# Two attentions of a fused three-layer block: a pair's sums over the values move one step later, between a step's scores and its turning

## The chip, the cores and the metric

The program runs on one core of one Trainium2 chip. The metric is the device time of one execution in microseconds (us). An execution is some 2.1 ms long, and the two attentions that the change touches take 75 us and 82 us of it.

## What is computed

The reference is a chain of three transformer layers on one sequence of 512 positions of width 1024, all in float32. The first layer has a sparse attention with 8 query heads of 64 over 2 groups of keys, a retention and an MLP. The second has an mLSTM, the third a softmax attention with 16 heads of 64 and a gate (called fox), and both have a feed-forward part. Two of its attentions count here:

```python
# first layer: selected blocks (with 8 blocks all are selected) and a window of 512, so both are causal attention
ss = jnp.einsum('qghd,gqkd->gqhk', qi, k_sel).astype(jnp.float32) * scale
p_s = jax.nn.softmax(jnp.where(smask, ss, NEG), axis=-1)
o_s = jnp.einsum('gqhk,gqkd->qghd', p_s.astype(dt), v_sel)
...
# third layer
logits = jnp.einsum('bqhd,bkhd->bhqk', qi, k).astype(jnp.float32)
logits = logits + (ci[..., :, None] - c[..., None, :])
p = jax.nn.softmax(jnp.where(mask, logits, -jnp.inf), axis=-1)
return jnp.einsum('bhqk,bkhd->bqhd', p.astype(v.dtype), v)
```

## The kernel before

Activations lie transposed in SBUF (128 features by 512 positions a tile). Weights stream in and are split in a high and a low part, and a product is three matmuls (L409 to L411). Each engine has one written-out order of instructions, and the engines are tied by counting semaphores. No planner decides anything: the order in the text is the order of issue.

Both attentions are one function, `attention` (L1110). The first layer's is called at L1632 (below: the first attention, 148 to 223 us of the trace), fox's at L2698 (1618 to 1700 us). The work of one attention is cut into 8 **pairs** of heads, and each pair into 4 **units**: unit i of a pair (i = 0 to 3) has the 128 queries of block i, and the (i + 1) x 128 keys that they may see, for both heads e = 0, 1 of the pair. So there are 32 units, of widths 128, 256, 384 and 512 in turn. A unit goes through these hands:

- `score` on TensorE (L1166, in fox also L2686, and L1171 for the mask): scores of both heads into two PSUM banks. Four banks serve two units, so `score(u)` waits until the exponentials of unit u - 2 have read theirs (`probs_ready`). With i = 0 it also waits for the split queries (`staged`).
- `maximum` on VectorE (L1230): the negated row maximum, one instruction a head.
- `exponential` on ScalarE (L1296): exp with the row sum beside it, one activation and one reading of the accumulator a head.
- `weigh` on VectorE (L1237, L1244 in the first attention, L1242 in fox): the probabilities times the reciprocal row sum.
- `turn` on TensorE (L1183): i + 1 transposes a head into one of two banks. It waits for `weighted`, and for ScalarE's copy of the last unit out of the same bank.
- `copy` on ScalarE (L1308, L1306): the turned probabilities into SBUF.
- `values` on TensorE (L1196): once a pair, after its unit i = 3, sixteen matmuls that sum over the values. It waits for the pair's last copy.
- `take` on VectorE (L1631 in the first attention, where two pairs add up in one bank and only every second pair is taken, L2681 in fox): the sums out of PSUM.

Once a pair, in the step with i = 0, ScalarE makes the high part of the next pair's queries (in fox of the keys too) at L1273, and VectorE the low part at L1213. In fox ScalarE also copies the values of a pair into `total` or `inv` (`stage_values`, L1288), and waits there for the sums of the pair before last.

The software pipeline is in `steps`: in step s each engine runs its `step` function once, and `unit(d)` is unit s - d. ScalarE's step is, in this order: the high parts (if i = 0), `copy(s - 3)`, `exponential(s)`, `stage_values`. VectorE's is `maximum(s)`, the low parts (if i = 0), `weigh(s - 1)`, then `take`. A step is named below by the width of its score: the 128 step is the one with i = 0.

Of the kernel before, what the change touches and what calls it, by code (L numbers as in the profile page):

```python
# [183 lines left out]
def build(nc, io, at):  # L184
    top = ExitStack()
    with top:
# [181 lines left out]
        def finish(spec):  # L368
            for b in range(spec.blocks):
                slot = (stream["slot"] + b) % 2  # L370
                raw_loaded[slot].n += 16
            stream["slot"] = (stream["slot"] + spec.blocks) % 2
            for t in (hi_ready, lo_ready, products_done):
                t.n += spec.blocks
# [735 lines left out]
        def attention(turns_n, q_of, k_of, v_of, static, space, factor, finish, together, lent, probs, free, key_bias=None, ends=None):  # L1110
# [12 lines left out]
            def turned_keys(p, e, j):  # L1123
                return probs_t[p][e][:, j, j * P:S] if j < 3 else probs_t[p][e][:, 1, 0:P]
# [12 lines left out]
            def prob(u, e):  # L1137
                return probs[2 * (u % 3) + e]

            def column(x, u, e):  # L1140
                return x[u % 3][:, e:e + 1]

            def steps(lag, step):
                for s in range(units + lag):
                    step(s, lambda lead: s - lead if 0 <= s - lead < units else None)

            def last_of(u):
                return u is not None and u % U == U - 1

            def tensor(pe):  # L1150
                def score(u):
                    n, i = u // U, u % U
                    w = (i + 1) * P
                    q, k = held[n]
                    half = [slice(64 * e, 64 * e + 64) for e in range(2)]
                    out = [score_bank[2 * (u % 2) + e] for e in range(2)]
                    if u < 2:

                        pe.wait_ge(evacuated.sem, b_e - 1 + u)
                    if i == 0:  # L1160
                        pe.wait_ge(staged.sem, b_st + once + each * (n + 1))
                    if u >= 2:
                        pe.wait_ge(probs_ready.sem, b_p + 2 * (u - 1))
                    for a, b in ((0, 0), (0, 1), (1, 0)):
                        for e in range(2):
                            pe.matmul(out[e][:, 0:w], q[a][half[e], i * P:w], k[b][half[e], 0:w],  # L1166
                                      start=a == 0 and b == 0, stop=False)
                    if key_bias is not None:
                        key_bias(pe, out, n, w)
                    for e in range(2):  # L1170
                        last = pe.matmul(out[e][:, i * P:w], ident_b[:, :], bias_b[:, :], start=False, stop=True)  # L1171
                    last.then_inc(scores_ready.sem, 1)

                def turn(u):
                    if u == 0:
                        pe.wait_ge(rows_out.sem, b_ro)
                        pe.wait_ge(cmp_dve.sem, b_cd)
                    for e in range(2):
                        pe.wait_ge(weighted.sem, b_n + 2 * u + e + 1)
                        if u >= 1:  # L1180
                            pe.wait_ge(probs_copied.sem, b_c + 2 * u + e - 1)
                        for j in range(u % U + 1):
                            last = pe.transpose(turn_bank[e][:, j * P:(j + 1) * P], prob(u, e)[:, j * P:(j + 1) * P], ident)  # L1183
                        last.then_inc(probs_turned.sem, 1)

                def values(u):
                    n, p = u // U, u // U % 2
                    pe.wait_ge(probs_copied.sem, b_c + 2 * u + 2)
                    if n >= 2:
                        pe.wait_ge(out_done.sem, b_d + (n // 2 if together else n - 1))  # L1190
                    out = out_bank[0 if together else p]
                    vals = v_of(n) if static else v_st[p]
                    for j in range(TT):
                        for e in range(2):
                            rows = slice(64 * e, 64 * e + 64)
                            last = pe.matmul(out[rows, j * P:S], vals[:, j, rows], turned_keys(p, e, j),  # L1196
                                             start=j == 0 and not (together and p == 1),
                                             stop=j == TT - 1 and not (together and p == 0))
                    last.then_inc(out_ready.sem, 1)

                def step(s, unit):
                    if unit(0) is not None:
                        score(unit(0))
                    if unit(3) is not None:
                        turn(unit(3))
                    if last_of(unit(4)):
                        values(unit(4))
                steps(5, step)

            def stage_low(dve, n):  # L1210
                for r, (st, src) in enumerate(stagings(n)):
                    dve.wait_ge(high_staged.sem, b_hi + once + n * each + r + 1)
                    dve.tensor_tensor(st[1], src, st[0].bitcast(F32), ALU.subtract).then_inc(staged.sem, 1)  # L1213
# [9 lines left out]
            def vector(dve):  # L1223
                def maximum(u):
                    w = (u % U + 1) * P
                    dve.wait_ge(scores_ready.sem, b_s + u + 1)
                    for e in range(2):
                        if u >= 3:
                            dve.wait_ge(probs_ready.sem, b_p + 2 * u + e - 5)
                        dve.tensor_reduce(column(neg_max, u, e), score_bank[2 * (u % 2) + e][:, 0:w], AX_X, ALU.max,  # L1230
                                          negate=True).then_inc(max_ready.sem, 1)

                def weigh(u):
                    n, i = u // U, u % U
                    w = (i + 1) * P
                    dve.wait_ge(probs_ready.sem, b_p + 2 * u + 2)
                    dve.reciprocal(row_sum[u % 3][:, :], row_sum[u % 3][:, :])  # L1237
                    dve.drain()  # L1238
                    for e in range(2):
                        x, scale = prob(u, e)[:, 0:w], column(row_sum, u, e)  # L1240
                        if factor is None:
                            ins = dve.tensor_scalar(x, x, scale, None, ALU.mult)  # L1242
                        else:
                            ins = dve.tensor_scalar(x, x, scale, factor(n, e, i), ALU.mult, ALU.mult)  # L1244
                        ins.then_inc(weighted.sem, 1)

                def take(u):
                    n, p = u // U, u // U % 2
                    if together and p == 0:
                        return  # L1250
                    if ends is not None and n == pairs - 1:
                        ends(dve)
                    dve.wait_ge(out_ready.sem, b_o + n + 1)
                    finish(dve, n, out_bank[0 if together else p]).then_inc(out_done.sem, 1)

                def step(s, unit):
                    if unit(0) is not None:
                        maximum(unit(0))
                        if s % U == 0 and s // U + 1 < pairs:
                            stage_low(dve, s // U + 1)  # L1260
                    if unit(1) is not None:
                        weigh(unit(1))
                    if last_of(unit(5)):
                        take(unit(5))
                steps(6, step)

            def stage_high(act, n):
                if n == 1:
# [58 lines left out]
            out_ready.n += pairs  # L1327
            out_done.n += turns_n if together else pairs
            return {"tensor": tensor, "vector": vector, "scalar": scalar}, begin_act, begin_dve

        def region(off, *shape):
# [1450 lines left out]
```

## Time and profile before

| what | value |
|---|---|
| median of 3 runs | 2143.31 us (2141.17 to 2144.65) |
| the profiled execution's own time | 2142.03 us |
| its span, first to last instruction | 2140.2 us |
| TensorE (PE) busy | 2066.3 us, 97% |
| VectorE (DVE) busy | 1220.8 us, 57% |
| ScalarE (ACT) busy | 795.5 us, 37% |
| mean granted TensorE clock | 0.987 |

The page's shares are means over some two dozen stages. Most of the span is streamed dense products that keep TensorE busy without a gap, and they hide that in the two attentions ScalarE and VectorE are busy nearly all the time too. For a change in the attentions the timelines of these stretches have to be read.

### The profile page before, as it was taken

Reading aid. Unit: us, or ns where it says so; the run is one execution under the profiler, and the core shown is the slowest. Engines: PE = TensorE matmul, PEld = TensorE weight load, DVE = VectorE, ACT = ScalarE, POOL = GpSimd, SP = SyncE. Lnnn points to the kernel's source line nnn. Section 1 sums busy time; section 2 is a strip of 40 time slices with the busy share of each in tenths; the row PEclk is TensorE's granted clock in tenths of the full one; section 3 lists DMA queues with packets and bytes.
Section 4 is the critical chain, followed back from the end, with each engine's and each line's share of the span. In section 5 each row is a group of like instructions: output and inputs, shape, how many; then the busy total and the mean of one; then the engine's idle time right before and its main releaser. Section 6 shows DMA issues by size and latency. Waiting matters only on the chain.

```text
span 2140.2 us, 25567 instructions
## 1 busy us (share of the span) xinstructions
PE 2066.3 (97%) x9936; PEld 1674.0 (78%) x9944; DVE 1220.8 (57%) x1719; ACT 795.5 (37%) x1236; POOL 21.3 (1%) x45
## 2 busy tenths in 40 slices
PE   7899999999999999999999999999999999999996
PEld 6776778888888888877788888878786678888885
DVE  5669645455444355456575564663537757647375
ACT  4239243232212133245343342442427734323242
POOL 1000000000000000000000000000000000000000
PEclk9989999999999999999999999999999999999998
DMA  4410412222222222321122223222220022222221
GB/s 168 158 60 1 128 50 93 104 99 99 99 98 99 99 98 77 120 89 59 60 98 98 98 79 113 70 94 89 99 99 21 21 79 79 98 98 98 99 83 54
DMA packets 34240, 188.52 MB, mean 88 GB/s; under 512 B 4440, under 2 KB 8696, under 8 KB 14400
## 3 DMA queue, kind: packets, MB, share of 16 engines
q1 hardware_dynamic: 31296, 179.41, 23.8%
q0 software_dynamic: 1696, 5.72, 1.0%
q10 hardware_dynamic: 1152, 2.10, 0.3%
q8 instruction: 62, 1.02, 0.2%
q14 instruction: 34, 0.28, 0.0%
HBM read 182.54 MB, written 2.11 MB: 86 GB/s over the span
## 4 chain that ended last, share of the span: by engine, by line
PE 88%; DVE 5%; ACT 2%; issue 1%; DVEq 1%; PEld 1%; DMA 1%; PEldq 0%; POOL 0%; SPq 0%; ACTq 0%; POOLq 0%
PE bank L409 23%; PE bank L411 23%; PE bank L410 23%; PE bank L486 4%; PE bank L491 4%; PE bank L487 4%; PE bank L1196 2%; PE bank L1166 1%; PE bank L645 1%; DVE w_lo L357 1%; PE bank L2205 1%; PE bank L1183 1%; ACT w_hi L343 1%; PE bank L2197 1%; DVEq L1238 0%
## 5 line engine op out<-in xcount | busy, mean ns | idle before, releaser
L343 ACT ACTIVATE w_hi<-w_raw 128x2048 fp32r<-128x2048 f32 (+3 forms) x174 | 314.4, 1807 | 812.0 <-PE bank L411 689.6
L409 PE MATMUL bank<-a_hi,w_hi 128*128 128x512 f32 x1376 | 540.3, 393 | 3.7 <-DVE shared L2546 1.6
L411 PE MATMUL bank<-a_hi,w_lo 128*128 128x512 f32 x1376 | 536.5, 390 | 0.0
L410 PE MATMUL bank<-a_lo,w_hi 128*128 128x512 f32 x1376 | 536.5, 390 | 0.0
L357 DVE TENSOR_TENSOR w_lo<-w_raw,w_hi 128x2048 fp32r<-128x2048 f32 (+3 forms) x174 | 374.8, 2156 | 143.7 <-ACT w_hi L343 143.5
L409 PEld LDWEIGHTS bank<-a_hi,w_hi 128*128 128x128 f32 x1376 | 258.9, 188 | 60.0 <-issue 3.4
L411 PEld LDWEIGHTS bank<-a_hi,w_lo 128*128 128x128 f32 x1376 | 258.8, 188 | 54.2
L410 PEld LDWEIGHTS bank<-a_lo,w_hi 128*128 128x128 f32 x1376 | 259.0, 188 | 53.3 <-issue 0.2
L409 PE MATMUL bank<-big_halves,w_hi 128*128 128x512 f32 x616 | 240.6, 391 | 3.1 <-DVE w_lo L357 3.0
L411 PE MATMUL bank<-big_halves,w_lo 128*128 128x512 f32 x616 | 239.8, 389 | 0.0
L410 PE MATMUL bank<-big_halves,w_hi 128*128 128x512 f32 x616 | 239.7, 389 | 0.0
L409 PEld LDWEIGHTS bank<-big_halves,w_hi 128*128 128x128 f32 x616 | 115.6, 188 | 29.7 <-DVE w_lo L357 5.9
L411 PEld LDWEIGHTS bank<-big_halves,w_lo 128*128 128x128 f32 x616 | 115.6, 188 | 24.2
L410 PEld LDWEIGHTS bank<-big_halves,w_hi 128*128 128x128 f32 x616 | 115.6, 188 | 23.8
L409 PE MATMUL bank<-w_hi,a_hi 128*128 128x512 f32 (+1 forms) x288 | 111.0, 385 | 3.0 <-DVE big L1676 1.0
L411 PE MATMUL bank<-w_hi,a_lo 128*128 128x512 f32 (+1 forms) x288 | 109.1, 379 | 0.0
L410 PE MATMUL bank<-w_lo,a_hi 128*128 128x512 f32 (+1 forms) x288 | 109.0, 379 | 0.0
L2546 DVE TENSOR_TENSOR shared<-bank,inv 128x512 f32<-128x512 f32 x88 | 56.6, 686 | 71.8 <-PE bank L411 71.5
L486 PE MATMUL bank<-a_hi,w_hi 128*128 128x512 f32 x176 | 74.3, 422 | 21.1 <-DVE w_lo L995 12.0
L2534 ACT ACTIVATE shared<-shared,conv 128x512 f32<-128x512 f32 x88 | 66.5, 803 | 34.1 <-DVE shared L2546 34.1
L2537 ACT ACTIVATE shared<-shared 128x512 f32<-128x512 f32 x44 | 27.9, 634 | 122.1 <-DVE shared L2556 122.1
L486 PE MATMUL bank<-big_halves,w_hi 128*128 128x512 f32 x184 | 72.2, 392 | 0.0
(340 smaller groups left out, 2432.6 us busy)
## 6 DMA issues: line engine op xcount, KB each, us to landing
w_raw<-in_w_fu SPq DMA_DIRECT2D x44, 1024.0 KB, 4.8
w_raw<-in_w_up SPq DMA_DIRECT2D x16, 1024.0 KB, 4.8
w_raw<-in_w_down SPq DMA_DIRECT2D x16, 1024.0 KB, 4.8
w_raw<-in_w_fd SPq DMA_DIRECT2D x16, 1024.0 KB, 4.8
w_raw<-in_w_fd SPq DMA_DIRECT2D x8, 768.0 KB, 4.3
w_raw<-in_w_rqk SPq DMA_DIRECT2D x4, 1024.0 KB, 5.0
w_raw<-in_w_rvg SPq DMA_DIRECT2D x4, 1024.0 KB, 5.0
w_raw<-in_w_gate SPq DMA_DIRECT2D x4, 1024.0 KB, 4.8
```

The costliest lines, as they stand in the source:

```text
L343: act.activation(w_hi[slot][:, cols], raw[slot][:, cols], ACT.Copy).then_inc(hi_half_ready.sem if half == 0 else hi_ready.sem, 1)
L357: ins = dve.tensor_tensor(w_lo[slot][:, cols], raw[slot][:, cols], w_hi[slot][:, cols].bitcast(F32), ALU.subtract)
L409: pe.matmul(out, w[0], x[0], start=first, stop=False)
L410: pe.matmul(out, w[0], x[1], start=False, stop=False)
L411: return pe.matmul(out, w[1], x[0], start=False, stop=last)
L486: pe.matmul(bank[2 * slot + c][:, :], w[0], x[0], start=k == 0, stop=False)
L487: pe.matmul(bank[2 * slot + c][:, :], w[1], x[0], start=False, stop=False)
L491: last = pe.matmul(bank[2 * slot + c][:, :], weights(slot, col)[0], x[1], start=False, stop=final)
L1196: last = pe.matmul(out[rows, j * P:S], vals[:, j, rows], turned_keys(p, e, j), start=j == 0 and not (together and p == 1), stop=j == TT - ...
L2534: act.activation(z[slot][:, c, :], u[slot][:, c, 2:S + 2], ACT.Identity, scale=tap(2, b, c), bias=tap(3, b, c)).then_inc(tapped.sem, 1)
L2537: act.activation(z[slot][:, 0, :], z[slot][:, 0, :], ACT.Gelu_apprx_tanh).then_inc(gelu_ready.sem, 1)
L2546: ins = dve.tensor_tensor(u[slot][:, c, 2:S + 2], bank[2 * slot + c][:, :], inv[:, :], ALU.mult)
```

## The change

The kernel's own time table in `step` is changed on two engines. On TensorE `values` was the last thing of a step, for the unit four behind the one just scored. Now it stands between `score` and `turn`, for the unit five behind. On VectorE `take` is one step later, six behind instead of five. Both loops get one step more at the end.

```diff
@@ tensor @@
                 def step(s, unit):
                     if unit(0) is not None:
                         score(unit(0))
+                    if last_of(unit(5)):
+                        values(unit(5))
                     if unit(3) is not None:
                         turn(unit(3))
-                    if last_of(unit(4)):
-                        values(unit(4))
-                steps(5, step)
+                steps(6, step)
@@ vector @@
                     if unit(1) is not None:
                         weigh(unit(1))
-                    if last_of(unit(5)):
-                        take(unit(5))
-                steps(6, step)
+                    if last_of(unit(6)):
+                        take(unit(6))
+                steps(7, step)
```

What this moves on TensorE in the first attention, at the end of a pair's 512 step (L1196 `values`, L1166 and L1171 `score`, L1183 `turn`):

```order
 L1171 MATMUL bank<-bias_b,ident_b 128x128 x2
 L1183 MATMUL bank<-const_sb,work 128x128 x2
+L1166 MATMUL bank<-big_halves 128x128 x6
+L1171 MATMUL bank<-bias_b,ident_b 128x128 x2
 L1196 MATMUL bank<-big,shared 64x512 x2
 L1196 MATMUL bank<-big,shared 64x384 x2
 L1196 MATMUL bank<-big,shared 64x256 x2
 L1196 MATMUL bank<-big,shared 64x128 x2
-L1166 MATMUL bank<-big_halves 128x128 x6
-L1171 MATMUL bank<-bias_b,ident_b 128x128 x2
 L1183 MATMUL bank<-const_sb,big 128x128 x4
```

The eight score matmuls of the next pair's 128 step now come before the sixteen of the sums, and the four transposes of unit i = 1 come after both. There are six such places in each attention (pairs 0 to 5). The sums of pair 6 stand in a step without a score: they move from behind the turning of unit 28 to before that of unit 29, which is the same place, and the last pair's sums stay last.

On VectorE in fox, before, from the low parts (L1213) of one pair's 128 step on:

```order
L1213 TENSOR_TENSOR a_lo<-big,a_hi 128x512 x2
L1237 RECIPROCAL row_sum<-row_sum 128x2
L1242 TENSOR_SCALAR a_plain<-a_plain,row_sum 128x512 x2
L2681 TENSOR_TENSOR big<-bank,big 128x512
L1230 TENSOR_REDUCE neg_max<-bank 128x1 x2
L1237 RECIPROCAL row_sum<-row_sum 128x2
L1242 TENSOR_SCALAR work<-work,row_sum 128x128 x2
L1230 TENSOR_REDUCE neg_max<-bank 128x1 x2
```

And with the change:

```order
L1213 TENSOR_TENSOR a_lo<-big,a_hi 128x512 x2
L1237 RECIPROCAL row_sum<-row_sum 128x2
L1242 TENSOR_SCALAR a_plain<-a_plain,row_sum 128x512 x2
L1230 TENSOR_REDUCE neg_max<-bank 128x1 x2
L1237 RECIPROCAL row_sum<-row_sum 128x2
L1242 TENSOR_SCALAR work<-work,row_sum 128x128 x2
L2681 TENSOR_TENSOR big<-bank,big 128x512
L1230 TENSOR_REDUCE neg_max<-bank 128x1 x2
```

The take (L2681) goes from before the 256 step's maximum to before the 384 step's. Nothing moves on ScalarE, GpSimd or the queue of SyncE.

## Rows read from the trace of the kernel before

**Rows 1.** The page: busy time, share of the span and instructions of each engine.

```profile
PE 2066.3 (97%) x9936; PEld 1674.0 (78%) x9944; DVE 1220.8 (57%) x1719; ACT 795.5 (37%) x1236; POOL 21.3 (1%) x45
```

**Rows 2.** Busy time by window: from the third pair's 128-wide score to the last pair's.

```profile
core 0: us, PE busy (x) PEld busy (x) DVE busy (x) ACT busy (x) POOL busy (x), PEclk, DMA share, GB/s
165.91:208.17 42.26, 40.94 (x342) 26.64 (x340) 38.08 (x108) 38.30 (x137) 0.00 (x0) 1.00 0.01 2
1635.13:1683.89 48.76, 45.18 (x377) 29.76 (x380) 40.93 (x115) 42.81 (x145) 0.00 (x0) 1.00 0.01 2
```

**Rows 3.** Timeline, first attention: start, duration, engine, instruction, count, [idle before <-releaser].

```profile
163.60 2.38 PE L1196 MATMUL bank<-big,shared 128*64 128x512 f32 x16
...
164.10 0.25 ACT L1296 ACTIVATION_READ_ACCUMULATOR work<-bank,neg_max 128x1 f32 x1
...
165.91 0.55 PE L1166 MATMUL bank<-big_halves 64*128 64x128 f32 x6
...
166.72 0.49 DVE L1230 TENSOR_REDUCE neg_max<-bank 128x1 f32<-128x128 f32 x2 [0.52 <-PE bank L1171]
166.94 0.66 ACT L1308 ACTIVATE shared<-bank 128x256 f32<-128x256 f32 x2 [0.36 <-PE bank L1183]
...
167.61 0.29 PE L1171 MATMUL bank<-bias_b,ident_b 128*128 128x128 bf16 x2
...
168.26 0.87 ACT L1308 ACTIVATE shared<-bank 128x384 f32<-128x384 f32 x2
...
168.88 0.75 DVE L1230 TENSOR_REDUCE neg_max<-bank 128x1 f32<-128x256 f32 x2
...
169.33 0.47 ACT L1296 ACTIVATE work<-bank,neg_max 128x256 f32<-128x256 f32 x1 [0.19 <-DVE neg_max L1230]
...
172.32 0.25 ACT L1296 ACTIVATION_READ_ACCUMULATOR work<-bank,neg_max 128x1 f32 x1
```

**Rows 4.** Timeline, first attention's last pair: its 128-wide score and its sums.

```profile
208.17 0.55 PE L1166 MATMUL bank<-big_halves 64*128 64x128 f32 x6
...
220.50 2.37 PE L1196 MATMUL bank<-shared 128*64 128x512 f32 x16 [0.86 <-ACT shared L1308]
```

**Rows 5.** Timeline, fox: pair 0's sums and what stands at their end.

```profile
1632.83 2.38 PE L1196 MATMUL bank<-fx_probs_t,total 128*64 128x512 f32 x16
1632.92 0.32 ACT L1296 ACTIVATION_READ_ACCUMULATOR work<-bank,neg_max 128x1 f32 x1
...
1635.13 0.33 PE L1166 MATMUL bank<-a_hi 64*128 64x128 f32 x2
```

**Rows 6.** Timeline, fox, one pair further on.

```profile
1642.58 2.37 PE L1196 MATMUL bank<-fx_probs_t,inv 128*64 128x512 f32 x16
...
1644.89 0.33 PE L1166 MATMUL bank<-a_hi 64*128 64x128 f32 x2
...
1646.03 0.73 ACT L1308 ACTIVATE fx_probs_t<-bank 128x256 f32<-128x256 f32 x2 [0.34 <-PE bank L1183]
...
1646.93 0.27 PE L1171 MATMUL bank<-bias_b,ident_b 128*128 128x128 bf16 x2
...
1647.87 0.88 ACT L1308 ACTIVATE fx_probs_t<-bank 128x384 f32<-128x384 f32 x2
...
1649.50 0.47 ACT L1296 ACTIVATE work<-bank,neg_max 128x256 f32<-128x256 f32 x1 [0.75 <-DVE neg_max L1230]
...
1650.57 0.50 PE L1166 MATMUL bank<-a_hi 64*128 64x512 f32 x2 [0.57 <-ACT work L1296]
...
1652.49 0.25 ACT L1296 ACTIVATION_READ_ACCUMULATOR a_plain<-bank,neg_max 128x1 f32 x1
```

**Rows 7.** Chain of waits in fox, merged: start, length, what (a steady pair's middle).

```profile
1645.81 0.29 DVE neg_max L1230
1646.30 1.20 DVE a_lo L1213 x2
1647.91 0.62 DVEq L1238
1648.53 0.60 DVE big L2681
```

**Rows 8.** Busy time by window: granted clock (PEclk) at the first attention's start and after.

```profile
147.00:158.00 11.00, 8.38 (x52) 5.49 (x51) 7.38 (x19) 6.47 (x19) 0.00 (x0) 0.71 0.01 2
...
166.00:225.00 59.00, 56.10 (x452) 36.65 (x453) 48.09 (x135) 49.60 (x173) 1.81 (x4) 1.00 0.02 5
```

## The prediction

> **What bounds the kernel now.** The page comes first: TensorE is busy 97% of the span [rows 1]. That is the mean of a kernel that is mostly dense products. The windows of busy time over the attentions say more: over five pairs TensorE is busy 40.94 of 42.26 us in the first attention and 45.18 of 48.76 us in fox, while ScalarE is busy 38.30 and 42.81 us [rows 2]. So TensorE waits 1.32 and 3.58 us there, some 0.26 and 0.72 us a pair, and ScalarE is close behind. Two engines at nine tenths mean that a loop through both decides, and for that I read the timelines.
>
> In fox the loop is plain. The sums run from 1642.58, and the next pair's 128 score can start only behind them, at 1644.89 [rows 6]. The chain of waits then goes over VectorE: maximum, low parts, weighing of unit 3, the take [rows 7]. Only then comes the 256 maximum, for which ScalarE has stood idle 0.75 us, and for its exponentials the 512 score has waited 0.57 us [rows 6]. After the 512 score come two transposes and the next sums, and the circle is closed: (1683.89 - 1635.13) / 5 = 9.75 us a pair. The first attention has the same circle with fewer instructions in it. ScalarE's wait for the 256 maximum is 0.19 us in a pair with no take before it [rows 3], and a pair takes 42.26 / 5 = 8.45 us [rows 2].
>
> **What the change does to the circle.** The sums (2.31 us from their start to the next start, 163.60 to 165.91 [rows 3]) leave the place ahead of the 128 score and go behind it, ahead of the turning of unit 1. No instruction is added. The 128 score is now held only by the 384 exponentials two units before, and VectorE's chain starts earlier. But the turning of unit 1 is late, ScalarE's copy of it waits, and queued behind that copy in the same in-order stream are the 128 exponentials and all that follow. So the new circle is: 128 score, sums, turning of unit 1, then ScalarE without a pause through copy 1, exponentials 128, copy 2, exponentials 256, copy 3, exponentials 384, which let the next 128 score go.
>
> *The first attention's steady pair.* From the 128 score's start to copy 1 it is 166.94 - 165.91 = 1.03 us now [rows 3], and 1.03 + 2.31 = 3.34 us with the sums between. ScalarE's string runs from 166.94 to the end of the 384 exponentials at 172.32 + 0.25 = 172.57, less the idle 0.19 us: 5.44 us [rows 3]. With 0.05 us for the signal that is 8.83 us. I take 8.8, since an idle time counts from the end of a record, and ScalarE's instructions otherwise start a little before the last one's record ends. Five pairs: 44.0 against 42.26, **+1.7 us**.
>
> *Its head.* The 128 score of the third pair starts at 165.91, behind the sums of the first. Without them it can start when the 384 exponentials are read, 164.10 + 0.25 + 0.05 = 164.40 [rows 3]: **-1.5 us**.
>
> *Its tail.* At the last pair's 128 score (208.17) the sums of pairs 0 to 5 are done today. With the change those of pair 5 are still to do, so from there to the end at 222.87 [rows 4] TensorE has 2.31 us more to do, and its only waits in the first half are of 0.1 to 0.3 us: **+2.1 us**. Together the first attention loses 2.3 us.
>
> *Fox.* Steady pair: copy 1 comes 1646.03 - 1644.89 = 1.14 us after the 128 score, with the sums 3.45. ScalarE's string from 1646.03 to 1652.74, less the 0.75 us of idle time that falls away, is 5.96 us [rows 6]. The sum with the signal is 9.46, and I take 9.4 by the same correction. Five pairs: 47.0 against 48.76, **-1.8 us**. Head: 1635.13 becomes 1632.92 + 0.32 + 0.05 = 1633.29 [rows 5], **-1.8 us**. Tail: 2.31 us of sums more, with TensorE without a wait, **+2.3 us**. Together fox gains 1.3 us.
>
> *The copy of values in fox.* ScalarE's `stage_values` waits for the sums of the pair before last. They now end only after the 128 score, but before the turning for which ScalarE has already waited in copy 1 of the same step. It costs nothing, and if the order were otherwise it would cost what copy 1 costs, once.
>
> *The take.* It waits for sums that end 3.1 us after the 128 score starts, and VectorE reaches it some 6 us after. Cost nothing. It leaves the way of the 256 maximum (0.60 us [rows 7]), and that is the reason why the 0.75 us in fox goes. What comes before the 384 maximum is unchanged in sum.
>
> *Outside.* The stages behind each attention shift with its end. No load is issued inside. Nothing.
>
> **Sum: +2.3 - 1.3 = +1.0 us.** Each half of that trade is worth more than the net. The profiled execution took 2142.03 us, its median over three runs is 1.3 us higher. I count from the middle, 2142.7, and forecast **2143.7 us**. A measurement here can tell some 0.2%, 4.3 us, from no change.
>
> *Bounds.* Low: TensorE never waits in the steady pairs. Then they give -1.3 and -3.6 instead of +1.7 and -1.8, and the sum is +1.0 - 3.0 - 1.8 = -3.8 us, 2138.9. High: ScalarE keeps its waits for the 256 maximum, 0.19 and 0.75 us a pair, on top of the new circle: 5 x (8.83 + 0.19) = 45.1 and 5 x (9.46 + 0.75) = 51.1, which is +2.8 and +2.3, and the sum is -1.5 + 2.8 + 2.1 - 1.8 + 2.3 + 2.3 = +6.2 us, 2148.9.
>
> *A rule against this working.* By occupancy TensorE is the fullest engine of the first attention, 40.94 us against ScalarE's 38.30 [rows 2], and by the timeline it is the circle through both that closes last. The Trainium skill (Perfetto Trace Analysis: Identifying the Most-Contended Engine) says to take the engine with the highest occupancy as the bottleneck, though it warns that matmul busy time is no good measure of TensorE. If that were all, the sums could stand anywhere in TensorE's order, and the first attention's steady pairs would gain their 1.3 us instead of losing 1.7.
>
> **The rivals.**
>
> 1. *TensorE is the bound in the first attention*, and ScalarE makes up for its late start. The new circle leaves TensorE only 8.8 - 8.2 = 0.6 us a pair idle, so this needs ScalarE's string to be 0.6 us shorter than its rows, which show it without a gap. Time: +1.0 - 3.0 = -2.0, 2140.7 us. Chance 0.10.
> 2. *The gain is whole in both*: rival 1, and the waits in fox go too, the low bound, 2138.9 us, which is just over 0.2% faster. For it speaks that fox's wait of 0.57 us for the exponentials is on the present circle. Against it, 5.96 us of ScalarE are in the new one. Chance 0.04.
> 3. *Slower: the maxima still come last.* Place: VectorE, L1230 at width 256. With the change the 256 score is done 2.31 us later, at 167.90 - 165.91 + 2.31 = 4.30 us after the 128 score's start, and the first half of the maximum takes about 0.4 us of the pair's 0.75, so 4.7. ScalarE asks for it when copy 2 ends, 3.34 + (169.13 - 166.94) = 5.5 us [rows 3]; in fox 5.0 against 6.2 [rows 6]. The slack is 0.8 and 1.2 us. If VectorE comes later than that (by the low parts and the weighing of unit 3 in front), the waits stay and the price is the high bound, 2148.9 us, 0.29% over. Chance 0.05.
> 4. *Slower: the clock falls.* At the start of the first attention the granted clock is 0.71 over 11 us, a part of them at 1.2 instead of 2.4 GHz, which costs up to 0.29 x 11 = 3.2 us; TensorE is busy 8.38 us of them. From 166 on it is 1.00 [rows 8], and in fox it stays 1.00 with 3.58 us of waits in five pairs [rows 2]. The new waits, 0.6 us a pair in the first attention, are no longer than fox's now. One fall in each attention would give 2143.7 + 6.4 = 2150.1 us. The Trainium skill (TensorE: Matmul & The Clock Gate, A second HAM failure mode) tells of a kernel whose frequent short idle times between groups of matmuls made the clock swing between its two levels. By that rule a fall would be likely; fox's rows speak against it. Chance 0.05.
> 5. *The change doesn't do what it says*: a wait elsewhere already orders sums behind the score. The waits of `values` are for copies and a take long done, and the order of the program shows the move. Under 0.01.
>
> **How the numbers follow.** Forecast 0.76, rival 1 0.10, both within 4.3 us of 2143.3. Rival 2 0.04, rivals 3 and 4 0.05 each. Faster by over 0.2% has 0.04, within 0.2% 0.86, slower 0.10. The range takes in both bounds: 2139 to 2149 us.
>
> **What would show it.** In the changed profile: the first attention some 2 us longer and fox 1 us shorter. Pairs of 8.8 us each in the first attention, no longer of alternating length, and of 9.4 us in fox. ScalarE's wait before copy 1 grows from 0.36 and 0.34 us to over 1 and some 0.7 us, and its wait for the 256 maximum is gone. TensorE waits some 0.6 us for the 384 exponentials before each 128 score of the first attention, and not before the 512 score. I am wrong if the first attention's pairs come under 8.5 us, if the 0.75 us waits in fox are still there, or if the granted clock leaves 1.00 between 166 us and the end of either attention.

## The result, and the profile after

| | before | changed |
|---|---|---|
| median of 21 runs each | 2143.31 us | 2146.96 us |
| ratio, 95% interval | | 1.0020 (1.0013 to 1.0026) |
| the profiled execution's own time | 2142.03 us | 2147.97 us |

The changed kernel is 3.65 us slower, 0.17%, with an interval of 2.8 to 5.6 us. That is inside the forecast's range and inside the band called no change, but it is not the forecast's +1.0 us, and the sign is clear of noise. By the page nothing of note has happened (to be held against [rows 1]):

```profile
span 2146.2 us, 25575 instructions
...
PE 2070.7 (96%) x9944; PEld 1674.8 (78%) x9944; DVE 1222.9 (57%) x1719; ACT 795.6 (37%) x1236; POOL 21.3 (1%) x45
```

The windows of busy time over the same five pairs say it. These answer to [rows 2]:

```profile
core 0: us, PE busy (x) PEld busy (x) DVE busy (x) ACT busy (x) POOL busy (x), PEclk, DMA share, GB/s
167.05:211.97 44.92, 41.25 (x340) 26.59 (x341) 39.44 (x109) 37.79 (x137) 0.00 (x0) 1.00 0.01 2
1639.10:1687.32 48.22, 46.69 (x380) 30.09 (x381) 41.33 (x116) 43.42 (x147) 0.00 (x0) 1.00 0.01 2
```

Five pairs of the first attention take 44.92 us instead of 42.26. TensorE's waits in them have grown from 1.32 to 3.67 us. Five pairs of fox take 48.22 us instead of 48.76, and TensorE's waits have shrunk from 3.58 to 1.53 us. Some 0.8 us of the 3.58 are no wait: in each of the five 512 steps the trace of before holds one of two matmuls of L2686, and a gap of 0.16 us in its place, so the real waits were some 2.8 us:

```profile
1651.69 0.38 PE L2686 MATMUL bank<-fx_parts,fx_sel 128*128 128x512 bf16 x1 [0.16 <-ACT fx_probs_t L1308]
```

The granted clock is 1.00 in both.

I cut each attention in three by its timeline: head (first score to the third pair's 128 score), five steady pairs, and tail (the last pair's 128 score to the end of its sums).

| us | head | five pairs | tail | sum of changes |
|---|---|---|---|---|
| first attention, before | 17.57 | 42.26 | 14.71 | |
| changed | 16.17 | 44.92 | 16.98 | |
| measured change | -1.40 | +2.66 | +2.27 | +3.5 |
| forecast | -1.5 | +1.7 | +2.1 | +2.3 |
| fox, before | 17.26 | 48.76 | 15.63 | |
| changed | 15.50 | 48.22 | 18.07 | |
| measured change | -1.76 | -0.54 | +2.44 | +0.1 |
| forecast | -1.8 | -1.8 | +2.3 | -1.3 |

The measured changes add to +3.7 us, which is the difference of the medians. (The two profiled executions differ by 5.9 us. The rest lies in stages that the change doesn't touch: the first attention starts at 150.88 instead of 148.34, 2.5 us later, and 0.3 us come back behind it.) Heads and tails came as forecast. Both steady pairs are some 0.2 us too long: 8.98 us for the forecast 8.8, and 9.64 for 9.4.

The timeline of one steady pair of the first attention, cut to what bears on the circle:

```profile
176.03 0.55 PE L1166 MATMUL bank<-big_halves 64*128 64x128 f32 x6 [0.72 <-ACT work L1296]
...
176.73 2.38 PE L1196 MATMUL bank<-shared 128*64 128x512 f32 x16
...
179.03 0.66 PE L1183 MATMUL bank<-const_sb,work 128*128 128x128 f32 x4
179.51 0.66 ACT L1308 ACTIVATE big<-bank 128x256 f32<-128x256 f32 x2 [1.43 <-PE bank L1183]
...
181.59 0.48 ACT L1296 ACTIVATE work<-bank,neg_max 128x256 f32<-128x256 f32 x1
...
184.62 0.24 ACT L1296 ACTIVATION_READ_ACCUMULATOR big<-bank,neg_max 128x1 f32 x1
...
185.01 0.44 PE L1166 MATMUL bank<-big_halves 64*128 64x128 f32 x4 [0.74 <-ACT big L1296]
```

The circle is the one that was forecast. TensorE scores, sums and only then turns. ScalarE has stood idle 1.43 us before copy 1 (0.36 before, [rows 3]). It then works without a wait through the 256 exponentials, where the 0.19 us wait for the maximum is gone, to the end of the 384 exponentials at 184.86, for which the next 128 score has waited 0.74 us. From 176.03 to 185.01 it is 8.98 us. Its TensorE part, score to copy 1, is 179.51 - 176.03 = 3.48 us where I had 3.34. ScalarE's string is 184.86 - 179.51 = 5.35 us where I had 5.44, and the step from 184.86 to 185.01 is 0.15 us where I had 0.05.

In fox the same lines (compare [rows 6]):

```profile
1648.74 0.33 PE L1166 MATMUL bank<-a_hi 64*128 64x128 f32 x2 [0.31 <-ACT work L1296]
...
1649.55 2.37 PE L1196 MATMUL bank<-fx_probs_t,inv 128*64 128x512 f32 x16
...
1652.33 0.73 ACT L1308 ACTIVATE fx_probs_t<-bank 128x256 f32<-128x256 f32 x2 [0.88 <-PE bank L1183]
...
1654.91 0.50 ACT L1296 ACTIVATE work<-bank,neg_max 128x256 f32<-128x256 f32 x1
```

The 0.75 us wait for the 256 maximum has gone, the 512 score waits no more, and copy 1 is reached 3.59 us after the score (forecast 3.45).

### The profile page after: what moved, and what is told of

Read it like the earlier page. It is cut to its first block, busy times and chain, and to the rows that moved or that the text cites. A ratio compares the mean times of both kernels' runs of the same rounds, so it can differ in the third digit from the quotient of the medians.

```text
span 2146.2 us, 25575 instructions
## 1 busy us (share of the span) xinstructions
PE 2070.7 (96%) x9944; PEld 1674.8 (78%) x9944; DVE 1222.9 (57%) x1719; ACT 795.6 (37%) x1236; POOL 21.3 (1%) x45
## 4 chain that ended last, share of the span: by engine, by line
PE 87%; DVE 4%; ACT 3%; PEld 3%; issue 2%; DMA 1%; DVEq 1%; PEldq 0%; POOL 0%; SPq 0%; ACTq 0%; POOLq 0%
PE bank L409 23%; PE bank L411 22%; PE bank L410 22%; PE bank L486 4%; PE bank L491 4%; PE bank L487 4%; PE bank L1196 2%; PE bank L1166 1%; PE bank L1183 1%; PE bank L645 1%; DVE w_lo L357 1%; PEld bank L409 1%; PEld bank L411 1%; PEld bank L410 1%; PE bank L2205 1%
```

## The experiments

Two theories went in. **The circle theory**: the whole change of the kernel's time is made inside the attentions, by the late turning of unit 1 and ScalarE's copy behind it. **The rivals**: the loss lies in other stages whose phase moves; or it is the take, late as well, that costs. Every kernel below has all of the computation. Pair times are means of five steady pairs, read from the timeline as above. Heads of the attention are left out of the comparisons of lengths where they differ. In every trace the granted clock falls to 0.50 some 3 to 6 us into the first attention's head, and in some it stays there for 10.3 us instead of 6.9. That costs 1.1 us more (the same order of the first attention has a head of 18.66 us in the fox-only kernel and of 17.57 us before).

### The change in one attention only

```diff
# first only, against the changed kernel
-                    if last_of(unit(5)):
+                    if static and last_of(unit(5)):
                         values(unit(5))
                     if unit(3) is not None:
                         turn(unit(3))
+                    if not static and last_of(unit(4)):
+                        values(unit(4))
...
-                    if last_of(unit(6)):
-                        take(unit(6))
+                    behind = 6 if static else 5
+                    if last_of(unit(behind)):
+                        take(unit(behind))
```

This is the change in the first attention alone (`static` is true there). The other kernel has the two conditions the other way round.

> The change in the first attention alone, fox as before. Circle theory (late turning of unit 1 starves ScalarE, and the pair's circle is 9.0 us): the first attention takes 78.1 us from its first score to the end of its last sums (before: 74.5), pairs of 9.0 us, fox stays at 81.6 us, the kernel is 3.5 us slower. Rival (the loss lies outside the attentions, in stages whose phase shifts): the first attention's +3.5 us stays, but the kernel's median need not follow; a median within 1 us of before would be for it.

> The change in fox alone. Circle theory: first attention 74.5 us, fox 81.8 us with steady pairs of 9.6 us (before 9.75) and a tail 2.4 us longer, the kernel within 0.5 us of before. Rival (loss outside): a median 2 us or more over before though both attentions keep their length.

| | first attention, pair | tail | fox, pair | tail | median | ratio to before |
|---|---|---|---|---|---|---|
| first only | 8.99 us | 16.99 | 9.75 us | 15.61 | 2146.35 us | 1.0013 (1.0004 to 1.0022) |
| fox only | 8.45 us | 14.71 | 9.64 us | 18.07 | 2142.62 us | 0.9999 (0.9990 to 1.0008) |

The kernel before stood at 2143.16 us in these comparisons. Each attention keeps, alone, the times it has in the changed kernel, and leaves the other's untouched. The whole loss is the first attention's (+3.2 of +3.65 us), and fox's part is a draw. The rival that puts the loss outside falls.

### The take alone, and the sums alone

```diff
# take alone, against before
-                    if last_of(unit(5)):
-                        take(unit(5))
-                steps(6, step)
+                    if last_of(unit(6)):
+                        take(unit(6))
+                steps(7, step)
```

> Only the take is one step later, the sums stay where they were. Circle theory: in the old circle the take's 0.60 us stands before the 256 maximum, on which ScalarE waits, so taking it out gains up to 0.6 us a pair in fox and in every second pair of the first attention: fox's pairs from 9.75 to 9.2 us and the attention 3 us shorter, the first attention 1 us shorter, the kernel 3 to 4 us faster than before. Rival (the late take is what cost time in the changed kernel, since it stands before the 384 maximum now): this kernel is slower than before, by up to 0.6 us for each of ten takes.

> Only the sums move, the take stays in the step that it was in, ahead of the 256 maximum. Circle theory: the maximum has 0.8 to 1.2 us to spare in the new circle, so the take's place is worth nothing: first attention 78.1 us, fox 81.8 us, the kernel like the changed one, 3.6 us slower than before. Rival (the take's move costs): 2 us or more faster than the changed kernel. Third outcome, the slack is not there: fox's pairs grow from 9.6 to 10 us or more.

With the take alone the pairs of fox take 9.15 us instead of 9.75, which is 0.60 us less. In the first attention they take 8.25 instead of 8.45: before, pairs of 8.22 and 8.81 us took turns, and now all are about 8.2 to 8.3. The median is 2139.21 us, a ratio of 0.9983 (0.9973 to 0.9992): **4.0 us faster than before**, at the upper end of what was expected. The windows of the two stretches show where it comes from:

```profile
165.63:206.89 41.26, 40.95 (x342) 26.64 (x340) 38.10 (x108) 38.31 (x137) 0.00 (x0) 1.00 0.01 2
1634.08:1679.84 45.76, 44.97 (x379) 29.79 (x382) 40.31 (x115) 43.09 (x145) 0.00 (x0) 1.00 0.01 2
```

TensorE's waits are 0.31 and 0.79 us in five pairs, where they were 1.32 and 3.58. The 0.79 us in fox are again five gaps of 0.16 us at L2686, each with a record missing. The last kernel below has the same order in fox and the same 9.15 us a pair, with all these records and 0.00 us of waits:

```profile
1633.34:1679.09 45.75, 45.75 (x382) 29.77 (x380) 40.29 (x115) 43.03 (x145) 0.00 (x0) 1.00 0.01 2
```

So 9.15 us is TensorE's own work for a pair of fox. That it lies just the take's 0.60 us under 9.75 is a coincidence: TensorE became the limit, with 0.22 us of ScalarE's wait for the maximum still there. In the timeline of fox the take now stands behind the 256 maximum, and ScalarE's wait for that maximum is 0.22 us instead of 0.75:

```profile
1655.94 0.75 DVE L1230 TENSOR_REDUCE neg_max<-bank 128x1 f32<-128x256 f32 x2
1656.39 0.48 ACT L1296 ACTIVATE a_plain<-bank,neg_max 128x256 f32<-128x256 f32 x1 [0.22 <-DVE neg_max L1230]
...
1657.24 0.68 DVE L2681 TENSOR_TENSOR big<-bank,big 128x512 f32<-128x512 f32 x1
```

With the sums alone moved the pairs take 8.99 and 9.63 us, like the changed kernel's 8.98 and 9.64, and the median is 2146.85 us, 1.0015 (1.0006 to 1.0024). In the new circle the take's place is worth nothing, as expected: ScalarE waits for no maximum in either kernel's steady pairs of fox. So the changed kernel consists of a move that gains 4 us by itself and one that loses 3.7 us whether the other is made or not. The gain does not add, because the second move takes the 256 maximum off the circle by itself.

### The sums behind the turning

```diff
# against the changed kernel
-                    if last_of(unit(5)):
-                        values(unit(5))
                     if unit(3) is not None:
                         turn(unit(3))
+                    if last_of(unit(5)):
+                        values(unit(5))
```

> The sums one step later as in the change, but behind the turning of unit 1 instead of before it: score, turning, sums. If ScalarE's starved copy alone makes the circle, its wait before copy 1 goes back to 0.4 us and the pairs of the first attention come to 8.5 us or less. If TensorE's own string from the sums to the turning of unit 3 (no gap in the changed kernel) is a circle of its own with the exponentials, the 256 score is now late by the same 2.3 us and the pairs come only to some 8.8 to 8.9 us (fox 9.5 instead of 9.64), the kernel some 1 us faster than the changed one and still 2.5 us slower than before.

The pairs took 8.84 and 9.50 us, the median was 2145.66 us, 1.0013 (1.0004 to 1.0022). That is the second outcome. Unstarving copy 1 gives back only 0.14 us a pair. The chain of waits of the first attention, from one 128 score on, shows TensorE's string:

```profile
173.92 0.55 PE bank L1166 x6
174.47 0.22 PE bank L1171 x2
174.69 0.45 PE bank L1183 x4
175.13 2.30 PE bank L1196 x16
177.44 0.55 PE bank L1166 x6
177.99 0.22 PE bank L1171 x2
178.20 0.66 PE bank L1183 x6
178.87 0.73 PE bank L1166 x6
179.59 0.22 PE bank L1171 x2
179.81 0.88 PE bank L1183 x8
180.69 0.89 PE bank L1166 x6
```

TensorE goes without a gap from the 128 score to the turning of unit 3 and the 512 score. ScalarE's timeline shows which turning it waited for, in the first attention and in fox:

```profile
178.57 0.88 ACT L1308 ACTIVATE big<-bank 128x384 f32<-128x384 f32 x2 [1.36 <-PE bank L1183]
...
1651.50 0.87 ACT L1308 ACTIVATE fx_probs_t<-bank 128x384 f32<-128x384 f32 x2 [0.51 <-PE bank L1183]
...
1653.54 0.28 ACT L1306 ACTIVATE fx_probs_t<-bank 128x128 f32<-128x128 f32 x1 [0.26 <-PE bank L1183]
```

In the first attention the starved copy is now that of unit 2, by 1.36 us, and from it ScalarE runs without a wait to the end of the 384 exponentials at 182.62, for which the next 128 score waits till 182.77. In fox ScalarE waits again before the copy of unit 3, so there the circle closes over that turning. A block of 2.3 us between the 128 score and the rest of the pair is late for whatever follows it, ahead of the turning or behind.

### The sums in two parts

```diff
# e6, against before, with the take late; values(u, blocks) runs only those key blocks
                     if unit(3) is not None:
                         turn(unit(3))
                     if last_of(unit(4)):
-                        values(unit(4))
+                        values(unit(4), (0, 1))
+                    if last_of(unit(5)):
+                        values(unit(5), (2, 3))
```

The other kernel has the second part between score and turning.

> The sums in two parts: key blocks 0 and 1 (eight matmuls, 1.55 to 1.6 us) in the old place behind the turning of the 512 step, blocks 2 and 3 (0.7 us) behind the next step's turning; take late as in the change. TensorE waits 0.72 us before each 128 score in the changed kernel, and by the circle theory the first part fills that wait and only 0.7 us stand in the way of anything: pairs of some 8.1 us in the first attention and 9.1 us in fox, the attentions 2.3 and 3.9 us shorter than before, the kernel 5 to 6 us faster than before. Rival (TensorE's own work is the bound at some 8.2 to 8.4 us a pair, and a second break in the sums costs a change of weights each time): no faster than with the take alone moved, 3 to 4 us faster than before.

> The same two parts, the second between the 128 score and the turning of unit 1, as the change has it. Circle theory: copy 1 is late by only 0.7 us plus the 0.14 us that a change from the mask's matmul to the sums and from the sums to the transposes was seen to cost, so pairs of 8.2 us in the first attention and 9.2 us in fox, 4 us faster than before. It tells what the place before the turning costs for itself, against the run with the second part behind it: 0.1 us a pair.

| | first attention, pair | fox, pair | median | ratio to before |
|---|---|---|---|---|
| second part behind the turning | 8.19 us | 9.27 us | 2139.42 us | 0.9983 (0.9974 to 0.9992) |
| second part ahead of it | 8.33 us | 9.42 us | 2138.71 us | 0.9980 (0.9971 to 0.9989) |

Both beat the kernel before, by 3.6 and 4.3 us (before: 2143.03). The first part fills TensorE's wait ahead of the 128 score. With the second part behind the turning TensorE has no wait left in either attention:

```profile
165.87:206.81 40.94, 40.94 (x343) 25.82 (x342) 38.43 (x108) 37.58 (x136) 0.00 (x0) 1.00 0.01 1
1633.82:1680.16 46.34, 46.34 (x382) 29.29 (x380) 40.94 (x116) 43.44 (x146) 0.00 (x0) 1.00 0.01 2
```

So 8.19 us is TensorE's own work for a pair of the first attention in this order, and the expected 8.1 lay under that bound. In fox the rival was right: 9.27 us of work a pair is more than the 9.15 that undivided sums reach. The timelines of fox show the price of the break: the two parts take 1.66 and 0.80 us to the start of what follows, 2.46 together, where the undivided sums take 2.30. The gain over the take alone is not there (expected 5 to 6 us, measured 3.6). By the pairs the part ahead of the turning is 0.14 us worse, by the medians 0.7 us better; executions of one kernel spread over more than that, and the pair times are the better measure. In the kernel with the second part ahead of the turning TensorE has no wait either (41.65 us busy in 41.65, and 47.09 in 47.09), so there this 0.14 us is TensorE's own time: the sums start 0.09 us later behind the score than the transposes do, and the four transposes behind them take 0.66 us instead of 0.61.

### Where the missing 0.2 us a pair comes from

```diff
# e8, against the changed kernel: the 128 score's waits in the other order
-                    if i == 0:
-                        pe.wait_ge(staged.sem, b_st + once + each * (n + 1))
                     if u >= 2:
                         pe.wait_ge(probs_ready.sem, b_p + 2 * (u - 1))
+                    if i == 0:
+                        pe.wait_ge(staged.sem, b_st + once + each * (n + 1))
```

> The changed kernel, with the 128 score's two waits in the other order, so that the wait for the split queries (long met) stands alone and the one for the exponentials is on the first weight load. In the changed kernel the score starts 0.14 us after the exponentials' record ends, where scores with one wait start 0.05 us after. If that is the second wait's own time in the sequencer, it goes from the circle: pairs of 8.9 instead of 8.98 us in the first attention, and the kernel up to 1 us faster than the changed one. If the 0.14 us is something else, the pairs stay at 8.98 us.

The pairs went from 8.98 to 8.89 us and from 9.64 to 9.55. The timeline shows why. The 384 exponentials end at 172.32 + 0.24 = 172.56, and the score starts 0.06 us later, not 0.15:

```profile
172.32 0.24 ACT L1296 ACTIVATION_READ_ACCUMULATOR work<-bank,neg_max 128x1 f32 x1
...
172.62 0.41 PEld L1166 LDWEIGHTS bank<-big_halves 64*128 64x128 f32 x6 [0.88 <-ACT work L1296]
172.62 0.55 PE L1166 MATMUL bank<-big_halves 64*128 64x128 f32 x6 [0.64 <-ACT work L1296]
...
173.32 0.65 PE L1196 MATMUL bank<-shared 128*64 128x512 f32 x2
```

Of two waits on one matmul one stands as an instruction of its own, and it cost 0.09 us when it was the one that came last. The median, 2146.22 us, is 1.0018 (1.0009 to 1.0027) of before: the 0.9 us expected of the swap is less than this comparison resolves.

The sums still start 0.70 us after the score (172.62 to 173.32), where the transposes used to follow after 0.61. Is it the wait on their first weight load?

```diff
# e9, against the changed kernel (values keeps the wait only in the last steps)
                 def step(s, unit):
+                    if last_of(unit(5)) and unit(0) is not None:
+                        pe.wait_ge(probs_copied.sem, b_c + 2 * unit(5) + 2)
                     if unit(0) is not None:
                         score(unit(0))
```

> The changed kernel, with the sums' wait for the last copy (long met) taken ahead of the 128 score, so that the sums' first weight load has no wait on it. In the changed kernel the sums start 0.70 us after the score's start, where the transposes used to start after 0.61 us. If that 0.09 us is the load held by its wait, it goes and the pairs of the first attention come to 8.9 us, unless the third wait ahead of the score costs as much there. If it lies in the change from the mask's bf16 matmul to float32 weights of 64 columns, the pairs stay at 8.98 us or grow.

> The same with the score's two waits swapped as well, so that both met waits stand ahead of the one that counts. With the swap alone the pairs were 8.89 us in the first attention and 9.55 us in fox. If the hoist gains 0.09 us: 8.80 and 9.46 us, which are the prediction's 8.8 and 9.4. If it gains nothing: 8.89 and 9.55 us again.

No. With the wait hoisted the pairs stay at 8.99 us (fox 9.64), and the sums still start 0.70 us after the score:

```profile
174.82 0.55 PE L1166 MATMUL bank<-big_halves 64*128 64x128 f32 x6 [0.74 <-ACT work L1299]
...
175.52 1.07 PE L1197 MATMUL bank<-shared 128*64 128x512 f32 x3
```

With hoist and swap the pairs took 8.94 and 9.60 us, worse than with the swap alone (8.89, 9.55), though without the swap the third wait ahead of the score had cost nothing (8.99 for 8.98). Why it costs 0.05 us only there is not shown. The medians were 2146.73 and 2145.50 us, beside 2143.80 for before. What makes sums start 0.09 us later than transposes behind the mask's bf16 matmul (the narrower float32 weights, or the order of loads) stays open. It is TensorE's spacing and no wait for another engine, as the kernel with the second part ahead of the turning showed.

### The best order for each

```diff
# e11, against before, with the take late
+                    now, later = ((0, 1), (2, 3)) if static else ((0, 1, 2, 3), ())
...
-                        values(unit(4))
+                        values(unit(4), now)
+                    if static and last_of(unit(5)):
+                        values(unit(5), later)
```

> For each attention the order that was best so far: in the first the sums in two parts behind the turnings (8.19 us a pair), in fox the sums in their old place with the take late (9.15 us a pair). Circle theory: nothing couples the two attentions, so the first takes 72.9 us (or 74 where the clock falls earlier in its head) and fox 78.6 us, 1.6 and 3.0 us less than before, and the kernel is 4 to 5 us faster than before, at 2138.5 us or so. If the attentions are coupled through the stages between them, the sum does not hold.

The first attention took 72.94 us and fox 78.62, with pairs of 8.19 and 9.15 us, as the parts had shown. The median is 2138.46 us, 0.9981 (0.9972 to 0.9990) of before and 8.5 us under the changed kernel. The two attentions are not coupled. Over the take alone the division gains some 0.4 us by the attentions' lengths (72.94 + 78.62 against 73.36 + 78.64), which no comparison of whole executions here could show.

## Why the prediction was right, and where its size was off

*The circle.* Right. The sums leave VectorE's chain, copy 1 is late, ScalarE runs through to the 384 exponentials, and the waits for the 256 maximum are gone. The pairs of the first attention no longer alternate in length. Moving the sums alone gave the same circle.

*Head and tail.* Right to 0.2 us each, four times.

*The steady pair.* This is the term that was mis-sized: "8.8" and "9.4" against a measured 8.98 and 9.64, ten pairs in all, 2.1 us of the 2.7 us that the forecast missed. The raw sums from the rows were 8.83 and 9.46. ScalarE's string did come out shorter than its rows, 5.35 us for 5.44 in the first attention and 5.91 for 5.96 in fox, so to round down for the overlap of records was right. The error was to carry the spacing of the old order into the new one. The signal was put at 0.05 us and measured 0.15, because the 128 score has two waits, and the one that now comes last is the separate one. The step from score to copy was put at 1.03 + 2.31 us and measured 0.14 us more (in fox too): the sums start 0.09 us later behind the score than the transposes did, and the transposes behind the sums take 0.05 us longer. The experiments showed the first of these, and left the second without a cause.

*The net.* The sum was small because two larger numbers stood against each other, +2.3 and -1.3 us. Errors of 1.2 and 1.4 us in them, both of one sign, made +1.0 into +3.65. The forecast time of 2143.7 us lies 3.3 us under the measured one, since it also counted from 2142.7 where the median of before is 2143.31. It had 0.86 on a change within 0.2%; by the medians the change is 0.17%, and the ratio of 1.0020 stands at the edge of that band. And fox did not become 1 us shorter, as "What would show it" has it: it took 81.79 us for 81.65.

*The take.* "Cost nothing" is right in the changed kernel. But the prediction gave its leaving as the reason why fox's wait of 0.75 us goes, and that step was wrong: with the sums moved and the take in its old place fox took the same 9.63 us a pair. The take's move was the half of the change that was worth making, and only in the old circle. The prediction did not price the halves apart.

*The bounds and rivals.* The low bound was too low by 0.6 us: it took all of fox's 3.58 us as waits, where five gaps are missing records. With TensorE's own work at 9.15 us a pair, five pairs can give back 48.76 - 45.75 = 3.0 us. That TensorE is the bound in the first attention (rival 1) was refuted for the changed order: TensorE waits 3.67 us in five pairs. It holds for the divided sums, where it waits 0.00. The Trainium skill (Perfetto Trace Analysis, Identifying the Most-Contended Engine) wants TensorE's headroom judged by its share of peak work and the busy share of its weight loads, not by the busy share of its matmuls. The prediction's "rule against this working" left that half out: the loads are busy 26.64 of 42.26 us [rows 2], less than ScalarE's 38.30, so that the loads' share doesn't make TensorE the fullest engine, in agreement with the outcome. The maxima did not come last (rival 3), and with the take left in its place there was still time to spare. The clock kept to 1.00 in both steady stretches, with waits of TensorE of 0.74 us in every pair of the first attention and 0.31 us in fox (rival 4).

## What to carry to other kernels

In a software pipeline over several engines, price each moved piece against the circle that it leaves and the circle that it enters, and each piece alone: here one of two moves that came together gained 4 us and the other lost as much. A long block on the engine that feeds everyone has no free place ahead of a short producer. Cut, it can fill a wait with as much as the wait holds, but only where TensorE does wait: that made the pair of the first attention 0.06 us shorter than the take's move alone, and the pair of fox 0.12 us longer. And where the net is a small difference of two larger terms, its error is theirs: tenths of a microsecond in a pair time, taken ten times, were more than the net.

## What the runs showed of the hardware

A matmul with two waits started 0.15 us after its last release when the separately issued wait was the one met last, and 0.06 us after when the wait on the weight load was (pairs shorter by 0.09 us in both attentions). At this place, which is on the circle, the order in which the two waits are written was worth 0.09 us a pair. A third wait, long met, ahead of the same matmul made the swapped kernel's pair 0.05 us longer (8.94 for 8.89), and left the unswapped one as it was (8.99 for 8.98).

Float32 sums with weights of 64 columns started 0.70 us after the 128 score's start, where float32 transposes started after 0.61 us, with and without a wait on the sums' first weight load.
